# One-core recurrent mixture layer in fp32: 64x64 level blocks, conditioning blocks moved, input matrices stored by units

## What is computed

```python
def chunk(state, inp):                      # chunks of 64 tokens, 4 heads of 128 channels
    qc, kc, vc, lf = inp
    bcum = jnp.cumsum(lf, axis=-2)
    o_inter = jnp.einsum('bhtd,bhde->bhte', qc * jnp.exp(bcum), state)
    diff = bcum[:, :, :, None, :] - bcum[:, :, None, :, :]
    pair_decay = jnp.exp(jnp.where(causal[:, :, None], diff, -jnp.inf))
    attn = jnp.einsum('bhtd,bhsd,bhtsd->bhts', qc, kc, pair_decay)
    o = o_inter + jnp.einsum('bhts,bhse->bhte', attn, vc)
```

## Time and profile before

| | |
|---|---|
| median of 3 runs | 1799.26 us |
| profiled execution, whole | 1801.19 us |
| its span, first to last instruction | 1799.4 us |
| PE busy (matmuls) | 1747.6 us, 97% |
| PE busy (weight loads) | 1010.8 us, 56% |
| DVE busy | 508.8 us, 28% |
| ACT busy | 261.2 us, 15% |
| DMA packets | 85232, 539.44 MB |

### The profile page before, as it was taken

One profiled execution on the slowest core, in us unless ns is written; L12 is line 12 of the kernel. 1 busy time (PEld: TensorE's weight loads), 2 busy tenths in 40 slices (PEclk: granted clock), 3 DMA queues, 4 the chain that ended last, 5 costly groups with the idle time before them and its releaser, 6 DMA issues.

```text
span 1799.4 us, 23413 instructions
## 1 busy us (share of the span) xinstructions
PE 1747.6 (97%) x9885; PEld 1010.8 (56%) x9885; DVE 508.8 (28%) x990; ACT 261.2 (15%) x433; POOL 26.7 (1%) x38
## 2 busy tenths in 40 slices
PE   8999999999999999999999999999999989999998
PEld 6677898888753333334343333333333337778885
DVE  2452377625451110111111111112010130006603
ACT  0322214100211111101011110101010121002200
POOL 1000000110000000000000000000000000000000
PEclk9999999999999999999999999999999999999999
DMA  9563332363569999999999999999999995542341
GB/s 320 215 234 116 118 117 103 104 207 142 221 242 396 429 433 430 432 431 431 430 426 436 424 435 427 434 427 429 429 432 429 433 368 184 167 141 94 124 157 42
DMA packets 85232, 539.44 MB, mean 300 GB/s; under 512 B 4903, under 2 KB 14421, under 8 KB 68145
## 3 DMA queue, kind: packets, MB, share of 16 engines
q1 hardware_dynamic: 79888, 528.54, 72.4%
q10 hardware_dynamic: 3472, 4.85, 1.0%
q0 software_dynamic: 1808, 5.11, 0.9%
HBM read 532.72 MB, written 5.77 MB: 299 GB/s over the span
## 4 chain that ended last, share of the span: by engine, by line
PE 84%; DMA 12%; DVE 2%; ACT 1%; issue 1%; SPq 0%; DVEq 0%; ACTq 0%
PE small L1282 21%; DMA arena<-in_expert_w_gu 11%; PE proj L688 10%; PE small L1319 9%; PE proj L1361 6%; PE proj L884 5%; PE proj L1449 4%; PE proj L1259 2%; PE small L1233 2%; PE small L1269 2%; PE small L957 2%; PE small L709 2%; PE small L1511 2%; PE proj L698 2%; PE small L1379 2%; PE small L1147 2%
## 5 line engine op out<-in xcount | busy, mean ns | idle before, releaser
L1282 PE MATMUL small<-arena 128*64 128x512 f32 x2048 | 449.6, 595 | 14.6 <-DMA arena<-in_expert_w_gu 12.2
L1282 PEld LDWEIGHTS small<-arena 128*64 128x64 f32 x2048 | 149.3, 137 | 299.5 <-issue 275.8
L1319 PE MATMUL small<-arena 128*64 128x512 f32 x1024 | 226.8, 595 | 8.8 <-ACT arena L1711 8.4
L688 PE MATMUL proj<-arena 128*128 128x256 f32 x832 | 185.8, 385 | 0.9 <-DMA arena<-in_w_in_first 0.9
L2348 DVE TENSOR_SCALAR arena<-small 128x512 f32<-128x512 f32 x32 | 22.1, 692 | 547.0 <-PE small L1289 547.0
L688 PEld LDWEIGHTS proj<-arena 128*128 128x128 f32 x832 | 159.4, 193 | 25.8 <-issue 3.0
L1319 PEld LDWEIGHTS small<-arena 128*64 128x64 f32 x1024 | 73.8, 137 | 139.7 <-issue 139.7
L1532 ACT ACTIVATE arena<-proj 128x512 f32<-128x512 f32 (+1 forms) x95 | 55.9, 595 | 532.4 <-PE proj L688 156.6
L1361 PE MATMUL proj<-arena 128*128 128x256 f32 x512 | 111.1, 379 | 0.0
L1361 PEld LDWEIGHTS proj<-arena 128*128 128x128 f32 x512 | 97.2, 190 | 13.7 <-issue 0.5
L1707 ACT ACTIVATE arena<-arena 128x512 f32<-128x512 f32 x32 | 20.2, 630 | 500.4 <-DVE arena L2348 500.4
(11 more groups left out here) (438 smaller groups left out, 1582.9 us busy)
## 6 DMA issues: line engine op xcount, KB each, us to landing
arena<-in_expert_w_gu SPq DMA_DIRECT2D x60, 4096.0 KB, 19.1
arena<-in_expert_w_down SPq DMA_DIRECT2D x64, 2048.0 KB, 15.7
arena<-in_w_in_first SPq DMA_DIRECT2D x20, 2048.0 KB, 8.3
arena<-in_w_in SPq DMA_DIRECT2D x16, 2048.0 KB, 8.8
arena<-in_expert_w_gu SPq DMA_DIRECT2D x8, 2048.0 KB, 10.9
arena<-in_w_ada SPq DMA_DIRECT2D x6, 2048.0 KB, 11.1
arena<-in_w_branch SPq DMA_DIRECT2D x4, 2048.0 KB, 8.6
arena<-in_w_out SPq DMA_DIRECT2D x4, 2048.0 KB, 8.1
```

The costliest lines, as they stand in the source:

```text
L688: mm = pe.matmul(ps[:, m * T:m * T + T], w[:, k, (2 * b + m) * P:(2 * b + m + 1) * P], XT[:, k, :], start=k == 0, stop=k == KD - 1)
L1282: mm = pe.matmul(bank[CAP * half:CAP * half + CAP, :], XG[:, k % 4, k // 4, :], w[:, k % 4, n * D + half * W:n * D + half * W + W], start= ...
L1319: mm = pe.matmul(y_bank[CAP * half:CAP * half + CAP, :], HM[:, m, u, :], w[:, m, half * W:half * W + W], start=u == 0 and m == 0, stop=u = ...
```

## The change

1. **Branch B in 64x64 blocks.** "B diag" and levels 0 to 5 compute only the 64x64 blocks on the diagonal of each tile and head, eight pairs that write to partitions 0 to 63 and 64 to 127 of one bank. Level 6 computes only the one 64x64 block that it needs, to partitions 0 to 63. DVE handles one bank for each level, and the 128-wide level masks leave the constants (896 columns, 458,752 bytes, less to load).
2. **Conditioning blocks moved.** "ada 1" to "ada 3" are loaded and used later: `ada_rows(1)` behind "C v", `ada_rows(2)` behind "C o", `ada_rows(3)` behind "B f", `ada(3)` behind "C col". "C if" and "C v" come one place forward in the ring.
3. **Low-rank products w and a** alternate between the lower and the upper 64 partitions.
4. **POOL** waits for "D xr 1" before it issues the four loads of WX and WAD, and for "C q 1" before the loads of WA2 and G2.
5. **Layout.** `by_units` stores `w_in_first` and `w_in_2` on the host so that a unit is one run of 16 KB for each partition.

```diff
+def by_units(w, widths):
+    rows = w.reshape(KD, P, -1).transpose(1, 0, 2)
+    ends = np.cumsum(widths)
+    return np.ascontiguousarray(np.concatenate([rows[:, :, e - n:e].reshape(P, KD * n) for e, n in zip(ends, widths)], 1))
...
-UNITS = (["D xr", "D gate", "C q", "ada 0", "C k", "ada 1", "C if", "C v", "ada 2", "C o", "ada 3", "B f", "B q",
+UNITS = (["D xr", "D gate", "C q", "ada 0", "C k", "C if", "C v", "ada 1", "C o", "ada 2", "B f", "ada 3", "B q",
...
-         + [f"ada {i}" for i in range(4)] + ["C row 0", "C row 1", "C col"] + [f"C S {h}" for h in range(4)]
+         + [f"ada {i}" for i in range(3)] + ["C row 0", "C row 1", "C col", "ada 3"] + [f"C S {h}" for h in range(4)]
...
-                return w_in[:, col[name]:col[name] + W].rearrange("(k p) n -> p k n", p=P), (KD, W)
+                return w_in[:, KD * col[name]:KD * (col[name] + W)].rearrange("p (k n) -> p k n", n=W), (KD, W)
...
-            return ins["w_in_2"][0, :, COL2[name]:COL2[name] + W].rearrange("(k p) n -> p k n", p=P), (KD, W)
+            return ins["w_in_2"][:, KD * COL2[name]:KD * (COL2[name] + W)].rearrange("p (k n) -> p k n", n=W), (KD, W)
...
+            pool.wait_ge(sig("proj_full"), proj_no("D xr 1") + 1)
             for t_, name in ((WX, "lru_wx"), (WAD, "lru_wa")):
...
+            pool.wait_ge(sig("proj_full"), proj_no("C q 1") + 1)
             pool.dma_start(WA2[0:64, :], ins["rwkv_w2"][0]).then_inc(sig("w2_loaded"), 16)
...
             ada(0)
-            ada_rows(1)
             w = unit("C if")
...
             ones_tokens("C v")
+            ada_rows(1)
+            ones_channels("C o")
             ada(1)
             ada_rows(2)
-            ones_channels("C o")
+            ones_channels("B f")
             ada(2)
             ada_rows(3)
-            ones_channels("B f")
-            ada(3)
...
             mm.then_inc(sig("small_full"), 1)
+            ada(3)
             ones_channels("B q")
...
-            for j in range(TT):
-                ps = small(f"B diag {j}")
-                for h in range(4):
-                    mm = pe.matmul(ps[:, h * P:h * P + P], kB[:, h, j * P:j * P + P], qB[:, h, j * P:j * P + P], start=True, stop=True)
+            def blocks64(name, lhs, rhs):
+                ps = small(name)
+                for n in range(8):
+                    j, h = divmod(n, 4)
+                    for ch in range(2):
+                        lo = j * P + CH * ch
+                        mm = pe.matmul(ps[CH * ch:CH * ch + CH, n * CH:n * CH + CH], lhs[:, h, lo:lo + CH], rhs[:, h, lo:lo + CH], start=True, stop=True)
                 mm.then_inc(sig("small_full"), 1)
+            blocks64("B diag", kB, qB)
...
-                if l < 7:
-                    for j in range(TT):
-                        ps = small(f"B level {l} {j}")
-                        for h in range(4):
-                            e = eBs[l % 2][:, h, j * P:j * P + P]
-                            mm = pe.matmul(ps[:, h * P:h * P + P], e, e, start=True, stop=True)
-                        mm.then_inc(sig("small_full"), 1)
+                if l < 6:
+                    blocks64(f"B level {l}", eBs[l % 2], eBs[l % 2])
+                elif l == 6:
+                    ps = small("B level 6")
+                    for n in range(8):
+                        j, h = divmod(n, 4)
+                        e = eBs[0][:, h, j * P:j * P + P]
+                        mm = pe.matmul(ps[0:CH, n * CH:n * CH + CH], e[:, 0:CH], e[:, CH:P], start=True, stop=True)
+                    mm.then_inc(sig("small_full"), 1)
...
+            for i in range(2):
+                banks = [proj(f"A {nm} {i}") for nm in "wa"]
+                for m in range(2):
+                    for ps, lo in zip(banks, (0, 64)):
+                        mm = pe.matmul(ps[:, m * T:m * T + T], WA2[lo:lo + 64, (2 * i + m) * P:(2 * i + m + 1) * P], zmix[lo:lo + 64, 12, :],
+                                       start=True, stop=True)
...
-            low_rank("w", e2A, "rwkv_w0")
-            low_rank("a", aA, "rwkv_a0")
+            for i in range(2):
+                low_rank("w", e2A, "rwkv_w0", i)
+                low_rank("a", aA, "rwkv_a0", i)
...
-            for i in range(4):
+            for i in range(3):
                 ada(i)
...
             dve.nop().then_inc(sig("C_dist"), 1)
+            ada(3)
...
+            acc64, level64_ = (tB.rearrange("p a b -> p (a b)")[:, 512 * n:512 * n + 512].rearrange("p (a b) -> p a b", b=CH) for n in range(2))
+            do(TTn(acc64, tiles(full("B diag"), CH), along(c("eye64"), 8), ALU.mult), "small_out")
+            do(dve.memset(aB[CH:P, :, 0:CH], 0.0))
             def add_level(l):
+                ps = tiles(full(f"B level {l}"), CH)
+                if l == 6:
+                    do(dve.tensor_copy(aB[0:CH, :, CH:P], ps[0:CH]), "small_out")
+                    return
+                do(TTn(level64_, ps, along(c("level64", l * CH, l * CH + CH), 8), ALU.mult), "small_out")
+                if l < 5:
+                    do(TTn(acc64, acc64, level64_, ALU.add))
+                    return
+                for ch in range(2):
+                    rows_, cols = slice(CH * ch, CH * ch + CH), slice(CH * ch, CH * ch + CH)
+                    do(TTn(aB[rows_, :, cols], acc64[rows_], level64_[rows_], ALU.add))
```

More of the change, by code:

```diff
@@ L38, in _place @@
     at = 0
-    for name, n in (("ident", 128), ("headsum", 128), ("level", 7 * 128), ("strict64", 64), ("upper64", 64), ("eye64", 64),
+    for name, n in (("ident", 128), ("headsum", 128), ("strict64", 64), ("upper64", 64), ("eye64", 64),
                     ("upper", 128), ("strict", 128), ("ones", 256), ("eye32", 32), ("slot", 64), ("reset64", 256),
@@ L152 @@
          + ["D gx 0", "D gx 1", "D ga 0", "D ga 1"]
-         + [f"ada {i}" for i in range(4)] + ["C row 0", "C row 1", "C col"] + [f"C S {h}" for h in range(4)]
+         + [f"ada {i}" for i in range(3)] + ["C row 0", "C row 1", "C col", "ada 3"] + [f"C S {h}" for h in range(4)]
          + ["C num 0", "C num 1", "C den", "C yT 0", "C yT 1"]
          + [f"Wb D {i}" for i in range(4)]
-         + ["B diag 0", "B diag 1"] + [f"B level {l} {j}" for l in range(7) for j in range(2)] + ["B cross"]
+         + ["B diag"] + [f"B level {l}" for l in range(7)] + ["B cross"]
          + ["B o 0", "B o 1", "A kk 0", "A kk 1"] + [f"A NT {i}" for i in range(2)]
@@ L908, in _ @@
             pe.wait_ge(sig("A_tanh"), 1)
[L909 to L915, removed]
+            for i in range(2):
[4 more added lines that the diff above has]
+                                       start=True, stop=True)
+                        if m == 1:
+                            mm.then_inc(sig("proj_full"), 1)
+            for i in range(2):
+                ps = proj(f"A g {i}")
+                for m in range(2):
+                    mm = pe.matmul(ps[:, m * T:m * T + T], G2[:, (2 * i + m) * P:(2 * i + m + 1) * P], zmix[:, 13, :], start=True, stop=True)
+                mm.then_inc(sig("proj_full"), 1)
             pe.wait_ge(sig("A_kksq"), 1)
@@ L1587, in _ @@
             do(act.activation(e2C, e2C, ACT.Ln), "C_ln")
+            channels("C o", oC, ACT.Sigmoid)
             ada_rows(2)
-            channels("C o", oC, ACT.Sigmoid)
-            ada_rows(3)
             act.wait_ge(sig("C_conv"), 1)
@@ L1594, in _ @@
             channels("B f", fB0)
+            ada_rows(3)
             act.wait_ge(sig("C_dist"), 1)
@@ L1641, in _, with low_rank @@
             gates("C", 1, (0,))
-            def low_rank(nm, dst, bias):
-                for i in range(2):
-                    n = proj_no(f"A {nm} {i}")
-                    act.wait_ge(sig("proj_full"), n + 1)
-                    for m in range(2):
-                        op = act.activation(dst[:, 2 * i + m, :], proj_bank[n % 4][:, m * T:m * T + T], ACT.Sigmoid,
-                                            bias=pv(bias, 2 * i + m, 2 * i + m + 1))
-                    op.then_inc(sig("proj_out"), 1)
-            low_rank("w", e2A, "rwkv_w0")
-            low_rank("a", aA, "rwkv_a0")
+            def low_rank(nm, dst, bias, i):
+                n = proj_no(f"A {nm} {i}")
+                act.wait_ge(sig("proj_full"), n + 1)
+                for m in range(2):
+                    op = act.activation(dst[:, 2 * i + m, :], proj_bank[n % 4][:, m * T:m * T + T], ACT.Sigmoid,
+                                        bias=pv(bias, 2 * i + m, 2 * i + m + 1))
+                op.then_inc(sig("proj_out"), 1)
+            for i in range(2):
+                low_rank("w", e2A, "rwkv_w0", i)
+                low_rank("a", aA, "rwkv_a0", i)
             for i in range(2):
@@ L1987, in differences @@
                 if l > 1:
-                    dve.wait_ge(sig("small_full"), small_no(f"B level {l - 2} 1") + 1)
+                    dve.wait_ge(sig("small_full"), small_no(f"B level {l - 2}") + 1)
                 do(TTn(e_right, right, ref, ALU.subtract))
@@ L2042, in shifted @@
```

(15 more changed lines are left out.)

9 lines of the change are left out of this document (3 added, 6 removed), and 4 rows, old and new, of the table PROJ.

## The result

The changed kernel takes 1790.65 us in the median of five runs (1789.49 to 1791.47), beside 1799.26 us before (1798.69 to 1800.44): 8.6 us less, a ratio of 0.995 with a 95% interval of 0.9938 to 0.9962. The forecast was 1791.2 us.

A forecast was written before the change was run, and what follows sets the result against it. PE was taken to bound the kernel, busy 97% of the span. Savings of 4.3 + 0.93 + 1.9 + 1.0 = 8.1 us took 1799.26 us to 1791.2 us, with a range from 1788.5 to 1796.0 us.

The forecast's parts named there:

- What bounds the kernel: Whole kernel: PE, busy 97%; PE work cut in the first block shortens the end equally while DVE, ACT and loads keep distance.
- Branch B: "B diag" and seven levels as 64x64 blocks, 0.0287 us a record plus 0.37 us form change: 4.3 us saved.
- Rival (a): Branch B: the two halves' weight loads don't overlap, a loss of 2.1 us there, 1797.5 us in all; 7%.
- The sum: Branch B's upper bound: 0.0574 us a record plus form changes, 16.4 us against 14.25 us before.
- Rival (b): Branch B: load and matmul on the same rows follow one another, 0.108 us a record, 1809.7 us in all; 4%.
- turning point of 0.064 us: Branch B: cost per record above which the change as a whole becomes a loss.
- Rival (c): Second block: long runs of `w_in_2` land late; landing doubled to 17.6 us costs 33 us, 1824 us in all; 3%.
- Low-rank products: Products w and a alternating halves: 16 records take 1.97 us, not 2.90 us; 0.93 us saved, 0.6 if the wait stays.
- Conditioning blocks: First block: "C v" loaded earlier, so PE's wait there ends, with the same PE work moved; 1.9 us saved.
- The start: First 20 us: POOL's later loads remove the 0.88 us wait and half of 0.2 us; 1.0 us, first 7.3 us unchanged.
- It stays: First block: the 1.2 GHz stretch near 130 us, costing 1.7 us, neither vanishes nor lengthens when conditioning work moves.
- the sum's bounds: Limits around the total saving of 8.1 us, allowing for clock falls at 130 and 181 us, 1.7 us each.

The follow-up runs named there:

- turned order: Changed kernel with each level's 64x64 products written first all to the lower half of the bank, then all to the upper; 1797.61 us in one execution.
- blocks alone: Kernel before with only branch B's 64x64 blocks and the shorter constants; 1794.38 us, ratio 0.9968.
- low-rank products alone: Kernel before with only the low-rank products w and a alternating between halves; 1798.64 us, ratio 0.9991.
- conditioning blocks alone: Kernel before with only the conditioning blocks moved, 2 KB pieces kept; 1797.33 us in one execution.
- layout alone: Kernel before with only the two input matrices stored by units; 1799.39 us, ratio 0.9999.
- POOL's late loads alone: Kernel before with only POOL's waits ahead of its late loads; 1798.79 us, ratio 0.9996.
- changed kernel again: The changed kernel, unaltered, rerun as the mark on the same chip as later variants; 1791.27 us, ratio 0.9953 to the kernel before.
- without the layout: Changed kernel with both input matrices row-major again, a unit being eight 2 KB pieces per partition; 1790.98 us, ratio 0.995 to the kernel before.
- thin matmuls spread: Changed kernel with full work between thin matmuls: ada(3) between the banks of B q, C den in two halves; 1787.65 us, ratio 0.9934 to before.

## Why the prediction was right

**What bounds the kernel.** PE's work and its few waits, one for one: the experts' first gather starts 7.93 us earlier, the stretches behind the changed ones give back only 0.08 and 0.06 us of what was won, and no engine came late. DVE's distance at the levels and at "C_rows" held.

**Branch B, forecast 4.3 us, measured 4.51 us.** Diag with level 0 takes 224.31 - 222.30 = 2.01 us, forecast 2.21 us less the 0.19 us that the fill behind it bears; a level with its fill takes 8.19 us, forecast 8.20 us, before 8.69 us. Level 6 takes 1.07 us, forecast 1.29 us with the same 0.19 us in it. The estimate went by the pace of 64x64 tiles that differ in rows and in columns, and took from L869 that tiles on the same rows overlap as well. Turning the order showed that this was the point on which the part depends, and it was right.

**Rival (a)** was priced with a pace of 0.0574 us for neighbours without overlap. The turned order runs at 0.057 us. Its loss against before is 0.55 us and not 2.1 us. The sum had 32 x 0.0574 + 0.17 = 2.01 us for a level without what its fill bears, and 1.83 us were measured: the change of form does not come on top. Where the records of one half meet those of the other, three of them start within 0.006 us of their neighbours instead of 0.058 us, which gives back about as much.

**Rival (b)** fell: a record costs 0.034 us with its form change in it (1.08 / 32), far below the turning point of 0.064 us. The Trainium skill, "TensorE: Matmul & The Clock Gate", section "The mechanism", has loads overlap running matmuls only where row groups differ. By that rule this would have been the outcome; all these blocks use the same 128 rows, and a record takes 0.034 us and not 0.108 us, so the measurement decides against it.

**Rival (c)** fell: a unit of the second matrix lands in 7.3 us in the changed kernel, sooner than the 8.8 us of the earlier trace rows.

**Low-rank products, forecast 0.93 us, measured 0.84 us** in the changed kernel and 0.83 us alone. The 16 records take 2.06 us, not 1.97 us.

**Conditioning blocks, forecast 1.9 us, measured 1.69 us.** The wait of 1.87 us went in full. Most of the difference is the moved work: one `ada_rows` took 1.74 us in its old place (74.20 - 72.46) and takes 1.85 us in the new one (90.77 - 88.92), and `ada(3)` takes 0.91 us where 0.88 us were the rule.

**The start, forecast 1.0 us, measured 1.03 us, and this is in part luck.** The step took the two waits, 0.88 us and half of 0.2 us, and held that the first 7.3 us stay. The waits went, but the first 7.3 us did not stay and the records at the low clock lasted longer. In the two profiled executions the first data come 7.34 - 6.54 = 0.80 us earlier, the waits give 0.88 + 0.17 us and the small steps between them 0.08 us, and the first 32 records take 9.68 us instead of 8.78 us, 0.90 us more: 1.03 us in all. Times in us, by trace; the records' time includes the wait within them, the landing counts from the issue, and the two traces with extra matmuls are left out:

| trace | first data | first 32 records | landing of the rest of "D xr" | second bank starts |
|---|---|---|---|---|
| before | 7.34 | 8.95 | 14.7 | 17.63 |
| blocks alone | 6.49 | 10.22 | 14.6 | 17.31 |
| low-rank products alone | 7.36 | 10.08 | 14.6 | 17.82 |
| conditioning blocks alone | 7.29 | 10.09 | 14.5 | 17.76 |
| layout alone | 7.12 | 9.30 | 15.2 | 17.94 |
| POOL's late loads alone | 7.30 | 9.93 | 10.5 | 17.61 |
| changed kernel | 6.54 | 9.68 | 10.2 | 16.60 |
| changed kernel again | 7.25 | 9.00 | 10.5 | 16.64 |
| without the layout | 6.67 | 9.74 | 10.4 | 16.80 |
| order turned | 6.46 | 9.33 | 10.1 | 16.18 |
| thin matmuls spread | 6.58 | 9.86 | 10.3 | 16.82 |

Three things can be read from it. POOL's late loads shorten the landing of the rest from 14.5 us and more to 10.5 us and less, in every trace, and with them PE never waits for it. That alone doesn't bring the second bank forward, since the first 32 records take from 8.95 to 10.22 us by the execution. And the first data come at 7.12 to 7.36 us in all five traces with the full constants, but at 6.46 to 6.67 us in five of the six with the shorter ones, which come with the blocks; the sixth, "changed kernel again", has 7.25 us. Neither the layout nor POOL's wait does that. Whether the shorter constants are the cause is open, as is why the slow records last longer in one execution than in another.

**The clock.** "It stays" was right for 130 and 181 us, which now are 128 and 179 us. The fall in the experts, 1.7 us, was missing from the sum's bounds, which counted only the two in the first block. Without it the profiled executions would lie 8.0 us apart; the medians lie 8.6 us apart.

## What to carry to other kernels

On this kernel, which is 97% PE, cutting fp32 products into 64-row blocks paid only when neighbours in the instruction stream write to different halves: 1.08 us a level in turn, 1.83 us in a row, 1.78 us uncut. A wait of PE in its first microseconds need not be worth its length: here the first 32 records, partly at 1.2 GHz, took 8.8 to 10.1 us for the same work by the execution, and in one kernel that took back a wait of 0.88 us. And a layout that speeds up loads which nothing waits for moves no time, however clean the loads look.

## What the runs showed of the hardware

Two tiles of 128 rows and 64 columns, with fp32 weights, overlap both their weight loads and their matmuls: 0.034 us a record in turn (level time over 32), 0.057 us in a row. The granted-clock column reads 1.00 in the first 13 us, though records of 256 columns start every 0.43 us there at first and every 0.216 us later: at the start it is the records that tell the clock. And the traces of these kernels have stretches at 1.2 GHz near 128, 179, 530, 1290 and 1470 us. None of the first four is in every trace; one near 1470 us is. At the first three a stretch of 3.4 us costs 1.7 us, and at the fourth it costs the end nothing. Any single profiled comparison of a few microseconds has to count them first.
